# Prologues of both blocks joined to the projections behind them, with 18 unread matmuls ahead of the transposes of each

## What is computed

```
first block, layer i = 0, 1:
    h = swiglu(rmsnorm(x, norm_pre[i,0]), ...);     x = x + 0.5 * rmsnorm(h, norm_post[i,0])
    h = s5 (i = 0) or conv (i = 1) of rmsnorm(x, norm_pre[i,1]);  x = x + rmsnorm(h, norm_post[i,1])
    h = swiglu(rmsnorm(x, norm_pre[i,2]), ...);     x = x + 0.5 * rmsnorm(h, norm_post[i,2])

second block, layer l = 0, 1:
    sh1, sc1, g1, sh2, sc2, g2 = split(silu(c) @ ada_w[l] + ada_b[l])
    y = retention(x*(1+sc1)+sh1) (l = 0) or nsa(x*(1+sc1)+sh1, shared) (l = 1)
    x = layer_norm(ALPHA * x + g1 * y, ln_g[l,0], ln_b[l,0])
    y = peer(x*(1+sc2)+sh2);   x = layer_norm(ALPHA * x + g2 * y, ln_g[l,1], ln_b[l,1])
    after layer 0:  kv_sh, kv_sc = split(silu(c) @ kv_ada_w + kv_ada_b)
                    shared = nsa_shared_kv(x*(1+kv_sc)+kv_sh, ...)
```

## Time and profile before

| | |
|---|---|
| median of 3 runs | 3871.84 us (3871.05 to 3873.94) |
| the profiled execution's own time | 3869.32 us |
| its span in the profile | 3867.5 us |
| mean granted TensorE clock | 0.911 of full speed |
| PE busy | 3306.5 us, 85% of the span |
| DVE, ACT, POOL busy | 64%, 43%, 31% |
| HBM traffic | 154 GB/s over the span |

### The profile page before, as it was taken

How to read it: one execution, slowest core, us unless ns; L and a number is a source line. 1 busy time by engine, 2 the same in 40 slices (tenths; PEclk the granted TensorE clock), 3 DMA queues, 4 the chain that set the end, 5 groups by cost and what they waited for, 6 DMA issues and landing times. The chain is left out here.

```text
span 3867.5 us, 64526 instructions
## 1 busy us (share of the span) xinstructions
PE 3306.5 (85%) x20412; PEld 2893.0 (75%) x20412; DVE 2491.1 (64%) x4701; ACT 1658.2 (43%) x3285; POOL 1181.4 (31%) x1077
## 2 busy tenths in 40 slices
PE   8978689898159897698899999976887979999997
PEld 7953589798049785498678999966666877899996
DVE  7979578685958544559954555554355986455555
ACT  4430344445134443244744444434343465444443
POOL 2526112120002200038863333320001977433333
PEclk9975799999679999899999999988678999999999
DMA  5520278685048553344055555554113413555564
GB/s 183 185 88 0 82 268 313 242 326 167 1 153 321 173 175 97 98 153 151 12 169 169 186 186 186 185 175 134 44 33 125 162 50 114 174 185 185 186 186 142
DMA packets 164581, 596.01 MB, mean 154 GB/s; under 512 B 18766, under 2 KB 19534, under 8 KB 164188
## 3 DMA queue, kind: packets, MB, share of 16 engines
q1 hardware_dynamic: 145264, 527.13, 41.5%
q10 hardware_dynamic: 19180, 67.22, 4.6%
HBM read 593.17 MB, written 1.11 MB: 154 GB/s over the span
## 5 line engine op out<-in xcount | busy, mean ns | idle before, releaser
L376 PE MATMUL ps<-hT,parts 128*128 128x256 f32 x12864 | 1615.2, 286 | 97.4 <-DVE parts L134 67.2
L376 PEld LDWEIGHTS ps<-hT,parts 128*128 128x128 f32 x12864 | 1600.3, 194 | 130.4 <-DVE parts L134 73.6
L134 DVE TENSOR_TENSOR parts<-ring,parts 128x512 fp32r<-128x512 f32 x1786 | 1185.8, 699 | 605.2 <-ACT parts L129 596.1
L129 ACT ACTIVATE parts<-ring 128x512 fp32r<-128x512 f32 x1930 | 1155.8, 628 | 619.9 <-PE ps L376 571.6
L376 PE MATMUL ps<-parts,gatedT 128*128 128x512 f32 x4128 | 1009.9, 397 | 7.6 <-DVE parts L134 7.6
L376 PEld LDWEIGHTS ps<-parts,gatedT 128*128 128x128 f32 x4128 | 761.1, 189 | 174.7 <-POOL gatedT L902 7.9
L1045 POOL TENSOR_TENSOR gatedT<-acted,iota 128x256 fp32r<-128x256 f32 x264 | 198.2, 751 | 1595.7 <-PE ps L376 1163.2
L1016 ACT ACTIVATE acted<-ps 128x256 f32<-128x256 f32 x264 | 102.1, 387 | 593.2 <-PE ps L376 593.2
L1048 POOL TENSOR_TENSOR gatedT<-acted,gatedT 128x256 fp32r<-128x256 f32 x264 | 311.2, 1179 | 20.7
L1029 DVE TENSOR_TENSOR acted<-acted,big 128x256 f32<-128x256 f32 x176 | 74.8, 425 | 359.7 <-ACT acted L1016 359.7
L376 PE MATMUL ps<-parts,hT 128*128 128x512 f32 (+2 forms) x1056 | 244.5, 395 | 65.9 <-DVE parts L134 65.9
(11 more groups left out here) (274 smaller groups left out, 2287.0 us busy)
## 6 DMA issues: line engine op xcount, KB each, us to landing
ring<-wts SPq DMA_DIRECT2D x965, 512.0 KB, 3.5
big<-mod_wts ACTq DMA_DIRECT2D x112, 512.0 KB, 4.7
big<-rows SPq DMA_DIRECT2D x15, 512.0 KB, 4.4
big<-mod_bias ACTq DMA_DIRECT2D x14, 512.0 KB, 4.8
big<-mod_rows SPq DMA_DIRECT2D x12, 512.0 KB, 6.3
big<-peer_keys SPq DMA_DIRECT2D x2, 1024.0 KB, 4.7
x<-x_in SPq DMA_DIRECT2D x1, 1024.0 KB, 5.0
big<-s_bc ACTq DMA_DIRECT2D x4, 256.0 KB, 3.4
```

The source lines that it names most:

```text
L129: act.activation(self.part(n, half, 0), self.raw(n, half), ACT.Copy).then_inc(self.hi_done, 1)
L134: v.tensor_tensor(self.part(n, half, 1), self.raw(n, half), self.part(n, half, 0).bitcast(F32), ALU.subtract).then_inc(self.lo_done, 1)
L376: last = pe.matmul(out, a(x), b(y), start=start and x + y == 0, stop=stop and x == 1)
```

## The change

- Five `to_columns`, `residual_rms` and three of the four `residual_ln` go. Their work moves into the stage of the projection behind them, as `ModEntry` (retention, both peers, `shared_kv`) and `SplitEntry` (nsa).
- In `ModEntry` PE transposes the *normalised* `x` itself. Modulation and, after a layer norm, its affine part become one scale and one offset for each feature, applied by ACT as it leaves PSUM (`value`), followed by ACT's rounding (`hi`) and DVE's subtraction (`lo`). The affine passes over `x` itself run on POOL behind the transposes.
- `shared_kv` also writes nsa's columns (`more_columns`), which `SplitEntry` only has to split.
- `ModSums` replaces `ModRows`: all rows are summed as columns (8 small matmuls for each), POOL makes gains and offsets, and only the four gates are stored as rows. The 14 early broadcast loads become `late` loads of 4 gates and 6 LN rows.
- `late` loads are issued at least eight tiles before the end of the stage, no longer behind the last tile.
- `WARM` goes from 0 to 18, in the five entries with `post` and in the four `ModEntry`.
- The stages ahead of each new entry split one tile ahead and load the root table (`ahead=1`).

The diff, cut to its core:

```
-WARM = 0
+WARM = 18
+GATES = (2, 5, 10, 13)
...
-        turns = (end - n) // RING
+        turns = (end - n - (2 * RING if late else 0)) // RING
...
+        for dst, src in late:
+            sp.dma_start(dst, src).then_inc(self.early, 16)
+            self.n_early += 16
         while n < end:
             load(n)
             n += 1
         self.issued = end
-        for dst, src in late:
-            sp.dma_start(dst, src).then_inc(self.early, 16)
-            self.n_early += 16
...
+class ModEntry:
+    def enter(self, s, block, first, done):
+        @block.scalar
+        def _(act):
+            for tt in range(TT):
+                if ln:
+                    act.wait_ge(s["e_squared"], tt + 1)
+                    act.activation(root(tt), aggr(tt)[:, 1:2], ACT.Sqrt, bias=k.eps[:, 2:3]).then_inc(s["e_rooted"], 1)
+                    if tt == 0:
+                        act.wait_ge(s["e_inverse"], 1)
+                        act.activation(k.x[:, 0, :], k.x[:, 0, :], ACT.Identity, scale=inv(0), bias=off(0)).then_inc(s["e_normed"], 1)
...
+            for n in range(done, 2):
+                k.w.split_hi(act, first + n)
+            for kc in range(KC + 1):
+                if kc < KC:
+                    act.wait_ge(s["e_turned"], kc // 2 + 1)
+                    act.activation(self.value(kc), self.turned(kc), ACT.Identity, scale=k.gain[:, self.norm, 0, kc:kc + 1],
+                                   bias=k.gain[:, self.norm, 1, kc:kc + 1]).then_inc(s["e_value"], 1)
+                if kc:
+                    act.wait_ge(s["e_value"], kc)
+                    act.activation(k.hT[:, 0, kc - 1, :], self.value(kc - 1), ACT.Copy).then_inc(s["e_hi"], 1)
...
+                gated(0)
+                moments(0)
+                gated(1)
...
+                moments(1)
...
+                v.tensor_scalar(k.x[:, 1, :], k.x[:, 1, :], aggr(1)[:, 0:1], inv(1), ALU.subtract, ALU.mult).then_inc(s["e_normed"], 1)
...
+            for kc in range(KC):
+                v.wait_ge(s["e_hi"], kc + 1)
+                v.tensor_tensor(k.hT[:, 1, kc, :], self.value(kc), k.hT[:, 0, kc, :].bitcast(F32), ALU.subtract).then_inc(s["e_lo"], 1)
...
+        @block.tensor
+        def _(pe):
+            warm(k, pe, first, WARM)
...
+        @block.gpsimd
+        def _(pool):
+            if ln:
+                pool.wait_ge(s["e_turned"], 4)
+                for n, op in ((1, ALU.mult), (2, ALU.add)):
+                    for tt in range(TT):
...
+                        pool.tensor_tensor(k.x[:, tt, :], k.x[:, tt, :], ln_row(k, n), op).then_inc(s["e_rows"], 1)
...
+class SplitEntry:
...
+            for n in range(done, 2):
+                k.w.split_hi(act, first + n)
+            for kc in range(KC):
+                act.activation(k.hT[:, 0, kc, :], src[:, kc, :], ACT.Copy).then_inc(s["e_hi"], 1)
...
-            lambda: ffn(k, 1, 1, Entry(k, 5, True, bias=True), mod_loads(k, mod_dst, 0, 6), beside=mods[2], ahead=0),
+            lambda: ffn(k, 1, 1, Entry(k, 5, True, bias=True), beside=mods[2]),
```

More of the change, by code:

```diff
@@ L242, in bc @@
     return ap.broadcast_to(shape)
[L247 to L310, removed]
@@ L707, in after @@
             evacuate(act, f, k.ps[:, 4 + f % 4, 0:T]).then_inc(s["stored"], 1)
+            if entry and isinstance(entry, ModEntry) and entry.more and f < KC:
+                entry.more_columns(act, s, f)
         splitting(k, block, first, n, after, entry=entry)
@@ L810, in tensor @@
         for n, (row, acc) in enumerate(self.rows):
+            for kc in range(KC):
+                last = pe.matmul(self.turned()[:, KC * n + kc:KC * n + kc + 1], acc[:, kc * P:(kc + 1) * P], k.ones[:, :],
+                                 start=True, stop=True)
+        last.then_inc(self.s["m_turned"], 1)
+        for n, (row, acc) in enumerate(self.gates):
             if n >= len(self.banks):
@@ L818, in scalar @@
         k = self.k
-        for n, (row, acc) in enumerate(self.rows):
+        act.wait_ge(self.s["m_turned"], 1)
+        act.activation(k.mod_cols[:, KC * self.first:KC * (self.first + len(self.rows))], self.turned(),
+                       ACT.Copy).then_inc(self.s["m_columns"], 1)
+        for n, (row, acc) in enumerate(self.gates):
             if n >= 1:
@@ L1412, in _ @@
             k.w.stream(sp)
+        @block.gpsimd
+        def _(pool):
+            mod.gpsimd(pool)
         @block.vector
@@ L1585, in retention, with peer @@
         rows_to_columns(k, out[:, :, h * D:(h + 1) * D])
-        project_rows(k, start=h == 0, stop=h == 1)
-    residual_ln(k, mod_row(k, 2), "ln_g00", "ln_b00")
-def peer(k, layer, sc, sh):
+        project_rows(k, start=h == 0, stop=h == 1, ahead=h, late=ln_loads(k, 2, "00") if h else ())
+def peer(k, layer, norm, late, ahead):
     big = k.big
@@ L1826, in peer, with other_columns, shared_kv @@
     held_downs(k, HELD, lambda f: weight(f + PK - HELD, 0))
-    gated_mlp(k, PK - HELD, 1, func, weight, start=False)
-def shared_kv(k, early):
+    gated_mlp(k, PK - HELD, 1, func, weight, start=False, ahead=ahead, late=late)
+def other_columns(k):
+    return k.big[:, 18432:20480].rearrange("p (c t) -> p c t", c=KC)
+def shared_kv(k):
     big = k.big
@@ L1849, in keep @@
         return act.activation(k.kT[:, f - 8, :], ps, ACT.Copy)
-    project_columns(k, 16, keep, early)
+    project_columns(k, 16, keep, entry=ModEntry(k, N_KV, more=(N_NSA, other_columns(k))))
     first = k.w.take(4)
```

229 lines of the change are left out of this document (144 added, 85 removed).

## The result

| | median of the runs | profiled execution |
|---|---|---|
| before | 3872.73 us (3871.05 to 3873.94, 4 runs) | 3869.32 us, clock 0.911 |
| after | 3826.84 us (3822.67 to 3831.06, 4 runs) | 3831.06 us, clock 0.915 |

The ratio is 0.9882, with a 95% interval of 0.9865 to 0.9899. The changed kernel is 46 us faster, where 79 were forecast. Its time lies outside the range, 16 us above the upper end of 3811. The sign was right, but 33 us, two fifths of the forecast gain, are missing.

A forecast was written before the change was run, and what follows sets the result against it. PE's matmuls bound the kernel (busy 85% of the span), so only its standing time could be saved: 68.6 + 8.6 + 2 = 79.2 us off 3869.3 gives 3790.1, with 2.5 for the median 3792 us; range 3778 to 3811.

The forecast's parts named there:

- The prologues of the second block: Five second-block entries, start to second evacuation: saves 14.3 (retention), 16.0 and 16.0 (peers), 16.3 (`shared_kv`), 6.0 (nsa), 68.6 us.
- the chain to row tile 1: Entries after a layer norm: row tile 1's normalisation done 10.0 us after the prologue's first instruction.
- ACT's pair: New entries: ACT's two instructions per chunk (`value`, `hi`) take 0.80 us, eight pairs 6.4 us; bounds 0.58 to 1.0.
- the last low part is half of an L134, 0.35 to 0.4: New entries: after ACT's eight pairs, only DVE's last low chunk adds time, 0.4 us in the sum.
- POOL slows the splitting: Rival, chance 0.12: POOL's passes behind three entries' transposes stretch L134 to 2.5 us, 5 us lost at each, 3807 us.
- The column sums: Conv's and retention's stages: about 112 small matmuls cost nothing, as DVE sets the pace and PE is free.
- The late loads: Stage ends before the five first-block entries: loads landed eight tiles earlier remove the excess wait, saving 8.6 us.
- The 18 matmuls: Entry starts: they speed the transposes by 0.4 us in each of five entries, 2 us; 0 to 3.5 for all.
- ACT's and DVE's chunks hide the clock behind the transposes: Entries, behind the transposes: ACT's and DVE's chunks set the pace, so PE's clock there doesn't matter.
- the clock is not held: Rival, chance 0.19: clock falls before the transposes, 2 us go, four `ModEntry` first tiles run at half clock; +8, 3800 us.
- slower than before: Rival, chance 0.03: added bursts bring half clock in long product stretches, about 160 us more; at mean 0.865 some 3885 us.

The follow-up runs named there:

- the mended kernel: Kernel after with POOL's passes cut in quarters and spread over the tiles behind the entry, and no column sums for the gate rows: 3795.25 us, ratio 0.9798.

## Why the prediction was wrong, step by step

- **The prologues of the second block, 68.6 us: 43.8 in the trace.** Retention (16.4 against 16.6 us) and nsa (14.6 against 14.5) were right. In the three entries with a layer norm the chain to row tile 1 and ACT's pair were right to 0.4 us, and the term "the last low part is half of an L134, 0.35 to 0.4" failed. The duration holds where POOL is idle (0.42 us), but the eight chunks met POOL's passes and took 11.4 us together, and the prediction had put POOL beside L134 only. Measured: 22.1 us for the three (26.2 by the gains). At the first peer the trace has 29.3 - 20.9 = 8.4 us. Part of it is the clock: after the starved stretch the products went on at the lower level until some 2 us before the second evacuation, where those of the kernel without passes were back at the upper one behind the low chunks. The row of the stretches of the kernel after (same columns as above):

```profile
1626.00:1640.00 14.00, 7.79 (x31) 6.94 (x32) 11.95 (x11) 5.11 (x14) 8.87 (x4) 0.50 0.07 20
```

- **The rival "POOL slows the splitting"** had the right engine and the wrong place. It priced L134 beside the passes and gave it 0.12, with the mean of 0.70 us as the argument against it. The mean of 1786 hid what one L134 does beside a long pass (up to 2.55 us when the passes were spread). And the passes start with the last transpose, and in that stretch DVE has the low chunks to do, on which PE waits directly. The row for it was there: DVE's normalisation took 2.95 us beside POOL and 0.81 without. That instruction has one tensor input only, so the row shows that the two engines meet and not for which operands. The Trainium skill, "GPSIMD Engine Reference", Specifications, says that the two contend when DVE has two SBUF inputs; L602 has two, and the trace agrees. The runs give the size: one instruction of DVE waits for one of POOL. No run varied the number of SBUF inputs. Not tried was to keep the chunk's value in PSUM, so that L602 had one SBUF input only.
- **The column sums, "nothing for them".** In retention's stage DVE set the pace only while PE's new work was shorter than DVE's 13.7 us. With the 64 and the gate sums it takes 18.1. Measured: 4.4 us in the trace, 5.7 and 7.2 between kernels. The step counted the matmuls and did not multiply them by a duration; 12.26/64 = 0.19 us each was the missing factor, though each has but one column. The count was half as well: the profile has two matmuls for each one written in the kernel, 224 at L867 for the 112. And most of them ran at the lower level of the clock (0.50 in the stretch above).
- **The late loads, 8.6 us: confirmed by themselves** (8.4 us in the kernel before, 8.7 us of PE's idle time in its trace). In the new kernel the same move carries more, 19.3 us, since the second block has late loads as well; that part is not a further gain, because the forecast's 68.6 already had them landed. In the first block the mean lead of the kernels with the move was 5.0 us at the retention prologue. The kernel before with the move alone, with its retention prologue at 1327.96, led by 7.2. Where these 2 us go was not settled.
- **The 18 matmuls, 2 us: nothing measurable** in three comparisons. They seemed to gain 2.3 us (or lose 1.8, by the gains), gain 1.8 and lose 2.0 us, all within the spread. The sentence that ACT's and DVE's chunks hide the clock behind the transposes was right. The rival "the clock is not held" was right about the clock in the entries with a layer norm and wrong about the price: in the mended kernel the first tile of an entry with a layer norm ran at the lower level, and the second evacuation was still at S + 20.9, since ACT's pairs set the pace. The Trainium skill, "TensorE: Matmul & The Clock Gate", Part 4, says that transposes don't count as work for the clock. The fall between the first and the second eight transposes of the mended kernel agrees with it, but PE also stood 1.71 us between them. Before retention the second eight and the first products stayed at the upper level (1.00), so the clock did not fall over sixteen transposes there. The runs don't separate the transposes from the pauses.
- **The sum.** 3826.8 - 22.1 (passes) - 7.2 (sums) = 3797.6, and the kernel with both mended has 3795.25, against the forecast of 3792. By the gains over the kernel before on the same chip it is 79.5 us, against the forecast of 79.2. That close an agreement is in part luck, since the 18 matmuls gave none of their 2 us. What is left is less than the chips differ by and isn't put down to any term. The range failed because the case of POOL carried 15 us at most and the sums none.
- **The rival "slower than before"** did not come (mean clock 0.915 against 0.911), but its arithmetic was off: 160 us more at half clock in 3867.5 us would take the mean from 0.911 to 0.89, not to 0.87.

## What to carry to other kernels

When a change moves work of one engine into a stretch that it did not share before, list for that stretch what every other engine runs in it, and look for a row of the profile in which the two met. An instruction of VectorE like those here (two operands in SBUF) that meets GpSimd is to be costed by the length of GpSimd's instruction. Cutting GpSimd's work to the slack of VectorE and placing it where VectorE has slack left no cost here; either alone got back half to two thirds. And "the other engine sets the pace there" is a comparison of two times: work out both, small instructions too, since a matmul of one column still cost 0.19 us, at a clock that had fallen.

## What the runs showed that was not expected

The exclusion works against GpSimd as well. In the stage behind the retention projections of the kernel without the gate rows' sums, a POOL operation on 128 x 8 elements, 0.20 us where DVE is idle, lasted 2.09 us and ended 0.06 us behind DVE's instruction. Timeline:

```profile
1489.78 2.28 DVE L1592 TENSOR_TENSOR big<-big 128x2048 f32<-128x2048 f32 x1
1490.03 2.09 POOL L908 TENSOR_TENSOR gain<-gain,cols 128x8 f32<-128x8 f32 x1
```

In `conv` it went further. In the kernel after POOL's small operation L902 (128 x 8 elements, 0.23 us once the taps were over) took 68.6 us, while DVE ran 240 taps (L1505) of 0.47 us without a pause, from 967.1 to 1062.2 us:

```profile
993.69 68.61 POOL L902 TENSOR_SCALAR gain<-mod_cols 128x8 f32<-128x8 f32 x1 [94.22 <-ACT mod_cols L880]
...
1062.53 0.23 POOL L902 TENSOR_SCALAR gain<-mod_cols 128x8 f32<-128x8 f32 x1
```

It ended when the taps did, and in all ten kernels with this code it took 66.6 to 75.4 us. Nobody waited for it here. No experiment was made on it, so that DVE's taps held it is read from the times alone. That it lasted over more than a hundred of DVE's instructions, while in the entries the two took turns, is open. The taps of 0.47 us started 95.1/240 = 0.40 us apart, so each overlapped the next; whether that left POOL no turn was not tested.
